# Sixteen early expert products in whole fp32, some of them issued between the groups of the gates

## The chip, the cores and the metric

The kernel runs on one core of a Trainium2 chip. The metric is the device time of one execution in microseconds; smaller is better. The program is one launch with about 49,000 instructions.

## The reference

The reference is a stack of two blocks, each applied with two layers, on 256 tokens of width 1024. Only the second half of a layer of the first block matters here, the product-key expert network (PEER). `h` are the normed tokens:

```python
q = (ht @ w_q).reshape(n_tok, PEER_HEADS, PEER_QDIM)      # 8 heads, 256 wide
s1 = einsum('thd,kd->thk', q[..., :half], sub_keys[0])    # 128 keys each
s2 = einsum('thd,kd->thk', q[..., half:], sub_keys[1])
# best 16 of each, best 16 of their 256 sums: 128 experts (key1*128+key2) for a token
gate = softmax(top)
act = gelu(einsum('td,thkd->thk', hc, expert_u[ec]))
y = einsum('thk,thkd->td', gate * act, expert_v[ec])
```

There are 128 x 128 experts. Each has a row of 1024 in `expert_u` and one in `expert_v`.

## The kernel before

The kernel gathers nothing. It computes a dense matrix of gates, `G` (expert by token, zero where an expert wasn't chosen), and then goes through all 128 blocks of 128 experts in each of the two layers. For a block `i` it computes the activations of all 256 tokens on TensorE (PE), applies gelu on ScalarE (ACT), multiplies with `G` on VectorE (DVE), and adds the product with the block of `expert_v` to `y_ps` in PSUM, where it stays over all blocks.

In the block loop every fp32 operand is split into a high part (fp32r) and a low part (the rest), and a product is three passes, high by high, high by low and low by high. So a block has these steps:

- `u_high` (ACT, line 1950) and `u_low` (DVE, line 2686) split the block of u, into one of two places of `utr`.
- `activations` (PE, line 1318): 8 parts of the width by 3 passes, 24 matmuls of 256 columns into one of two banks `prob_ps`.
- `gelu` (ACT, line 1967) and `weighted` (DVE, lines 2700 to 2704): gate, and the split into `wtr`.
- `v_high` (ACT, line 1977) and `v_low` (DVE, line 2711) split the block of v into `vr`.
- `combine` (PE, line 1330): 12 matmuls of 512 columns.

On PE the order is written out: activations of block i+1 stand ahead of combine of block i. The raw blocks are loaded by SyncE (SP), 512 KB each, into two places for u (`expert_u`) and two for v (`expert_v`), all four in the first half of the tile `slab`. SP waits for the low part of the last user of a place (`next_u`, `next_v`, `next_pair`).

Ahead of that loop come, in this order, the queries and scores of the heads, the search for the best keys on DVE, and the gates. The gates are made in 32 groups of 8 tokens: DVE writes the 8 gated one-hot rows and 1 plain one, POOL 4 plain ones and ACT 3 (`one_hot`, lines 1929 and 1931), PE multiplies them (line 1303, 8 fp32 matmuls of 128 columns, each seen as 2 records), and ACT copies the result to `G` (`gates_out`, line 1939). The rows and the result have two buffers. What DVE, POOL and ACT write for group n+2 waits until group n is full.

`EARLY = (0, 12)`: in layer 1 the activations of the first 12 blocks are made in another way. They are whole fp32 products, 8 matmuls of 256 columns each (line 1290, 16 records), without a split of u and h. Eleven of them stand on PE while DVE is still searching for the best keys, the twelfth stands behind the turning of the pairs (`turn_pairs`) and ahead of the gates. Gelu (line 1900) writes them to small tiles in `slab`, and behind the gates only the combines of these blocks are left, eleven of them in a row. v of blocks 1 and 3 have places of their own (`first_v`), the others share the two places. Layer 0 makes no product early; it starts its loop behind the gates.

In layer 0 PE computes the last two pieces of the modulation (line 1268) ahead of `turn_pairs`.

Of the kernel before, what the change touches and what calls it, by code (L numbers as in the profile page):

```python
# [1 line left out]

# [13 lines left out]
P = 128  # L16
D = 1024
S = 256
# [40 lines left out]
EARLY = (0, 12)  # L59

# [171 lines left out]
def two_blocks(nc, io, out):  # L232
    ctx = ExitStack()
    with ctx:
# [69 lines left out]
        ut_act = Signal(sem("ut_act"), a=NKEYS)  # L304
        ut_dve = Signal(sem("ut_dve"), a=NKEYS)
        am_full = Signal(sem("am_full"), a=NKEYS)
        gelu_done = Signal(sem("gelu_done"), a=NKEYS)
# [3 lines left out]
        v_in = [Signal(sem(f"v_in{q}"), a=NKEYS // PLACES, step=16) for q in range(PLACES)]  # L311
# [4 lines left out]
        early_in = [sem(f"early_in{q}") for q in range(EARLY[1] // 2)]  # L316
        early_full, early_done = sem("early_full"), sem("early_done")
        first_v_in = {i: sem(f"first_v_in{i}") for i in (1, 3)}
# [35 lines left out]
        small = sb("small", [P, 1024])  # L354
# [16 lines left out]
        first_v = {1: hT[:].rearrange("p k s -> p (k s)")[:, D:2 * D], 3: slab[:, 1, D:2 * D]}  # L371

        def early(i):

            at = 3 * D + i * S if i < 4 else (i - 4) * S
            return slab[:, 0, at:at + S]
# [7 lines left out]
        def v_raw(l, i, m):  # L384

            return first_v[i] if isinstance(i, int) and EARLY[l] and i in first_v else expert_v[:, m % 2]

        def v_landed(l, i, m, place):

            if isinstance(i, int) and EARLY[l] and i in first_v:  # L390
                return first_v_in[i], 16
            return v_in[m % 2].at("a", l, place + 1 - (2 if EARLY[l] and m % 2 else 0))
# [30 lines left out]
        assert sr.at <= 1024  # L423
# [50 lines left out]
        early_u = rb.take(EARLY[1] - 4, D)  # L474

        def early_rows(i):

            return early_u[:, i] if i < EARLY[1] - 4 else early_more[:, i - EARLY[1] + 4]
# [188 lines left out]
        def slabs_a(sp, l):  # L667
            if l == 0:
                sp.dma_start(cT, io["c_turned"]).then_inc(c_in, 16)
            for i, name in enumerate(SLABS["a"][l]):  # L670
# [6 lines left out]
                if l == 0:  # L677
# [7 lines left out]
                    if name == "wq3":  # L685
                        sp.wait_ge(t5_out, 16)
                        for h in range(8):
                            for t in range(T):
                                sp.dma_start(skewed[:, h, t, :],
                                             bass.AP(t5_dram.tensor, h * 512 + (P if t == 0 else 0), [[1, P], [1, S]]))\  # L690
                                    .then_inc(t5_skew, 16)
                    for s in {"ada3": (0,), "in1": (1, 2), "in3": (3, 4), "out1": (5, 6, 7), "wq3": (8,)}.get(name, ()):
# [3 lines left out]
            u = io["peer_u"][l]  # L696
            v = io["peer_v"][l].rearrange("(n p) d -> n p d", p=P)
            for q in range(EARLY[l] // 2):
                rows_q = early_u[:, 2 * q:2 * q + 2] if 2 * q < EARLY[l] - 4 else early_more[:, 2 * q - EARLY[l] + 4:][:, 0:2]
                sp.dma_start(rows_q, u[2 * q:2 * q + 2].rearrange("q p d -> p q d")).then_inc(early_in[q], 16)  # L700
            sp.wait_ge(*accs.full_at("a", l, "wq2"))
            sp.sem_inc(passed["sp"], 1)
            for q in range(PLACES):
                if not EARLY[l]:
                    sp.dma_start(expert_u[:, q], u[q]).then_inc(u_in[q].sem, 16)
                if q == 0 or not EARLY[l]:
                    sp.dma_start(expert_v[:, q], v[q]).then_inc(v_in[q].sem, 16)
            if EARLY[l]:
                sp.wait_ge(early_full, EARLY[l])
                sp.sem_inc(passed["sp"], 1)  # L710
                sp.dma_start(first_v[1], v[1]).then_inc(first_v_in[1], 16)
                sp.wait_ge(*gates_full.at("a", l, S // TOKG))
# [2388 lines left out]
```

## Time and profile before

| | |
|---|---|
| three timed runs | 3085.27, 3090.32, 3091.12 us |
| their median | 3090.32 us |
| profiled execution, first to last instruction | 3090.2 us |
| profiled execution, its own time beside the span | not recorded; the span is taken for it |
| PE, DVE, ACT, POOL busy | 96%, 64%, 43%, 9% |
| gates of layer 0 | 281.1 to 364.6 us |
| blocks of layer 0 | 364.7 to 1094.8 us |
| gates of layer 1 | 1344.6 to 1427.2 us |
| blocks of layer 1 | 1429.8 to 2119 us |

How to read it: times in rows are microseconds from the first instruction of the profiled execution. PE is the matmul side of TensorE, PEld its weight loads, which overlap; PEclk is the granted clock as a share of 2.4 GHz. A matmul's record reaches from its start to its modelled end, so that records of matmuls that follow each other overlap; the step from one to the next is the start of the next less its own. The chain follows the last instruction back to what released each, and its pieces abut.

### The profile page before, as it was taken

The numbers are of one execution on the slowest core, as the hardware profiler recorded it, in microseconds if no ns is written. First come the engines' busy times: TensorE is split into PE (matmuls) and PEld (weight loads), VectorE is DVE, ScalarE is ACT, GpSimd is POOL, SyncE is SP. The second block draws the span as 40 slices with busy tenths as digits, with TensorE's granted clock in tenths as the row PEclk, the third lists the DMA queues.
The fourth block names the chain that finished last, engine by engine and source line by source line (L and its number), as shares of the span: only waits on it lengthen the run. The fifth ranks groups of instructions, "written<-read, shape, count | busy, mean of one in ns | idle before, by whom it ended". The sixth has DMA issues, their size and how long they took to land.

```text
span 3090.2 us, 49370 instructions
## 1 busy us (share of the span) xinstructions
PE 2954.5 (96%) x17506; PEld 2574.5 (83%) x17506; DVE 1979.7 (64%) x3642; ACT 1319.7 (43%) x2114; POOL 274.9 (9%) x398
## 2 busy tenths in 40 slices
PE   8897899999999999988999999998999999999999
PEld 4684799999999876877999999998978898988897
DVE  4769866677777634797666666665656655555764
ACT  1245844444444412566444444444443434434433
POOL 0027600000000000473000000000000000000000
PEclk9899999999999998999999999999999999999999
DMA  8532156767666642303555565565334454423454
GB/s 328 199 115 82 54 185 219 234 227 231 225 231 231 211 149 82 144 8 97 190 185 185 196 195 192 189 195 190 108 133 164 162 179 155 176 109 143 160 181 150
DMA packets 130809, 524.33 MB, mean 170 GB/s; under 512 B 17981, under 2 KB 28093, under 8 KB 108025
## 3 DMA queue, kind: packets, MB, share of 16 engines
q1 hardware_dynamic: 120648, 508.13, 47.8%
q10 hardware_dynamic: 10034, 14.52, 1.4%
q8 instruction: 78, 1.28, 0.2%
q14 instruction: 49, 0.40, 0.0%
HBM read 519.44 MB, written 3.16 MB: 169 GB/s over the span
## 4 chain that ended last, share of the span: by engine, by line
PE 81%; DVE 8%; ACT 6%; DMA 1%; issue 1%; DVEq 1%; ACTq 1%; POOL 0%; SPq 0%
PE prob_ps L1318 22%; PE acc L1330 22%; PE acc L966 6%; PE acc L1549 6%; PE acc L1562 6%; PE acc L951 3%; PE acc L925 2%; PE acc L1496 2%; ACT arena L1939 2%; PE turn_ps L1074 2%; PE acc L904 2%; PE acc L1521 1%; ACT arena L1929 1%; PE acc L1048 1%; ACT slab L1931 1%
## 5 line engine op out<-in xcount | busy, mean ns | idle before, releaser
L1318 PEld LDWEIGHTS prob_ps<-hTr,utr 128*128 128x128 f32 x5856 | 734.4, 191 | 26.1 <-issue 8.3
L1318 PE MATMUL prob_ps<-hTr,utr 128*128 128x256 f32 x5856 | 745.5, 284 | 1.7 <-DVE utr L2686 1.2
L1330 PE MATMUL acc<-vr,wtr 128*128 128x512 f32 x2964 | 718.9, 391 | 1.2 <-DVE vr L2711 1.2
L1330 PEld LDWEIGHTS acc<-vr,wtr 128*128 128x128 f32 x2964 | 541.1, 189 | 104.3 <-issue 1.8
L2711 DVE TENSOR_TENSOR vr<-slab,vr 128x1024 fp32r<-128x1024 f32 x246 | 301.4, 1225 | 406.8 <-ACT vr L1977 406.6
L1977 ACT CAST vr<-slab 128x1024 fp32r<-128x1024 f32 x246 | 258.3, 1050 | 578.8 <-PE acc L1330 570.2
L2686 DVE TENSOR_TENSOR utr<-slab,utr 128x1024 fp32r<-128x1024 f32 x244 | 297.3, 1218 | 12.9 <-ACT utr L1950 12.9
L2240 POOL TENSOR_TENSOR small<-small 128x1 f32<-128x1 f32 (+4 forms) x29 | 26.2, 904 | 2666.2 <-DVE small L2303 1459.0
L1950 ACT CAST utr<-slab 128x1024 fp32r<-128x1024 f32 x244 | 255.5, 1047 | 8.2 <-DMA slab<-in_peer_u 3.4
L2961 DVE TENSOR_TENSOR slab_lo<-slab,w_hi 128x2048 fp32r<-128x2048 f32 x64 | 143.8, 2288 | 122.2 <-ACT w_hi L2206 122.2
L2206 ACT CAST w_hi<-slab 128x2048 fp32r<-128x2048 f32 x64 | 119.2, 1908 | 157.9 <-DMA slab<-in_pack_b 149.9
L1967 ACT ACTIVATE arena<-prob_ps 128x256 f32<-128x256 f32 x244 | 93.9, 385 | 209.8 <-PE prob_ps L1318 209.7
L2786 DVE TENSOR_TENSOR slab_r<-slab,arena_r 128x2048 fp32r<-128x2048 f32 (+1 forms) x52 | 115.7, 2258 | 86.7 <-ACT arena_r L2058 86.6
L1303 PE MATMUL acc<-slab 128*128 128x128 f32 x1024 | 130.2, 281 | 37.2 <-ACT slab L1931 29.6
L925 PE MATMUL acc<-hT,slab 128*128 128x256 f32 x704 | 159.5, 383 | 2.7 <-ACT hT L1598 1.4
L1562 PE MATMUL acc<-w_hi,uTr 128*128 128x512 f32 x512 | 157.8, 389 | 2.3 <-issue 2.3
L1303 PEld LDWEIGHTS acc<-slab 128*128 128x128 f32 x1024 | 120.4, 193 | 47.3 <-DVE slab L2679 43.4
L2263 POOL TENSOR_SCALAR slab<-iota,arena 128x128 f32<-128x128 f32 x256 | 152.9, 613 | 45.7 <-ACT arena L1604 32.7
L2675 DVE TENSOR_SCALAR slab<-iota,arena 128x128 f32<-128x128 f32 x512 | 152.9, 368 | 2.2 <-PE acc L1303 2.0
L925 PEld LDWEIGHTS acc<-hT,slab 128*128 128x128 f32 x704 | 132.7, 192 | 21.6 <-issue 3.6
L2350 DVE SCALAR_TENSOR_TENSOR arena<-arena,small 128x512 f32<-128x512 f32 x152 | 113.9, 749 | 16.6 <-DMA arena<-in_pack_a 8.4
L966 PE MATMUL acc<-arena_r,hT_hi 128*128 128x512 f32 (+2 forms) x320 | 122.8, 384 | 0.0
(310 smaller groups left out, 4179.4 us busy)
## 6 DMA issues: line engine op xcount, KB each, us to landing
slab<-in_pack_b SPq DMA_DIRECT2D x132, 1024.0 KB, 4.9
slab<-in_peer_v SPq DMA_DIRECT2D x255, 512.0 KB, 3.5
slab<-in_peer_u SPq DMA_DIRECT2D x244, 512.0 KB, 4.6
arena<-in_pack_a SPq DMA_DIRECT2D x84, 512.0 KB, 4.7
slab<-in_pack_a SPq DMA_DIRECT2D x40, 1024.0 KB, 7.0
arena<-in_peer_u SPq DMA_DIRECT2D x6, 1024.0 KB, 14.6
slab<-in_pack_b SPq DMA_DIRECT2D x4, 832.0 KB, 5.3
arena<-in_pack_a SPq DMA_DIRECT2D x2, 1024.0 KB, 18.3
```

What stands on the lines that cost most here:

```text
L925: ins = pe.matmul(dst, w(k, a, P), lhs[:, k, :], start=(k == 0), stop=(k == KD - 1))
L966: ins = pe.matmul(dst[:, t, 0:n], hT_r[hp][:, 4 * h + k, t * P:t * P + P], proj_operand(u0 + h, wp)[:, k, a:a + n], start=(h == 0 and k == ...
L1303: ins = pe.matmul(gate_ps[:, n % 2, q * P:q * P + P], rows[:, n % 2, 1, q, :], rows[:, n % 2, 0, q, :], start=True, stop=True)
L1318: ins = pe.matmul(prob_ps[:, m % 2, 0:S], utr[:, m % 2, uh, k * P:k * P + P], hTr[:, hh, k, :], start=(k == 0 and n == 0), stop=(k == KD - ...
L1330: ins = pe.matmul(y_ps[:, t, n, :], wtr[:, m % 2, wh, t * P:t * P + P], v[:, vh, n * 512:n * 512 + 512], start=first and k == 0, stop=last ...
L1549: ins = pe.matmul(acc[:, accs.buf("b", use), 2 * h + j, :], mlp_operand(u, wp)[:, k, j * P:j * P + P], hm_r[hp][:, k, :], start=(k == 0 an ...
L1562: ins = pe.matmul(acc_nat(accs.buf("b", f"dn{n}"))[:, t, :], uTr[:, up, 4 * j + k, t * P:t * P + P], mlp_operand(u, wp)[:, k, :], start=(j ...
L1950: act.copy(utr[:, m % 2, 0], expert_u[:, m % 2]).then_inc(ut_act.sem, 1)
L1977: act.copy(v_place(l, i)[:, 0], v_raw(l, i, m)).then_inc(v_hi.sem, 1)
L2263: ins = nc.gpsimd.tensor_scalar(rows[:, n % 2, 1, q, :], iota[:], pairsT[:, 1, tok:tok + 1], None, ALU.is_equal)
L2686: dve.tensor_tensor(utr[:, m % 2, 1], expert_u[:, m % 2], utr[:, m % 2, 0].bitcast(F32), ALU.subtract).then_inc(ut_dve.sem, 1)
L2711: dve.tensor_tensor(v_hl[:, 1], v_raw(l, i, m), v_hl[:, 0].bitcast(F32), ALU.subtract)\
```

## The change

`EARLY` becomes (12, 16): both layers make the activations of their first blocks as whole fp32 products. `AHEAD = (3, 12)` of them stand ahead of the gates. The last one (11 and 15) stands behind the gates. The rest, 8 in layer 0 and 3 in layer 1, are issued matmul by matmul behind the groups of the gates: 64 matmuls over 32 groups, two for each, and 24 over 32 (`gate_steps`). ACT does the gelu of such a block once its last matmul is issued, in the next group.

`LISTED = (0, 12)` blocks of u are loaded ahead in a list, as before; further ones go one by one through the two places of `expert_u`, each when the product two before it is done. The results of gelu have a tile of their own, `early_at`, for which the tile `small` is cut and the scratch for dynamic DMAs made smaller. The high and low parts of v of the early blocks alternate between both places of `utr`, but for the last, which goes to `vr`. For the raw v, the two places of `expert_u` are lent while the early blocks are combined, so that v has four places; only block `EARLY - 2` goes to place i % 2 of `expert_v`. All combines of early blocks stand in a row on PE, and the activations of the next block behind them.

The core of the diff:

```diff
-EARLY = (0, 12)
+EARLY = (12, 16)
+LISTED = (0, 12)
+AHEAD = (3, 12)
+def gate_steps(l, n):
+    total = (EARLY[l] - 1 - AHEAD[l]) * KD
+    return range(n * total // (S // TOKG), (n + 1) * total // (S // TOKG))
...
+        def v_home(l, i):
+            return i % 2 if i == EARLY[l] - 2 else i % 4
...
         def v_place(l, i):
-            if not isinstance(i, int) or i >= EARLY[l] or i % 2 and i != 3:
+            if not isinstance(i, int) or i >= EARLY[l] - 1:
                 return vr[:]
-            return utr[:, 0] if i == 3 else utr[:, 1]
+            return utr[:, 0] if i % 2 else utr[:, 1]
...
SyncE
+            def first_blocks(l):
+                sp.wait_ge(*accs.full_at("a", l, "wq2"))
+                sp.sem_inc(passed["sp"], 1)
+                for q in range(PLACES):
+                    sp.dma_start(expert_u[:, q], u[LISTED[l] + q]).then_inc(u_in[q].sem, 16)
+                for q in range(PLACES):
+                    sp.dma_start(expert_v[:, q], v[q]).then_inc(v_in[q].sem, 16)
...
+            for i in range(LISTED[l] + 2, EARLY[l]):
+                sp.wait_ge(*early_full.at("a", l, i - 1))
+                sp.sem_inc(passed["sp"], 1)
+                sp.dma_start(expert_u[:, i % 2], u[i]).then_inc(u_in[i % 2].sem, 16)
...
+            for i in (2, 3):
+                sp.wait_ge(*early_full.at("a", l, EARLY[l] - 3 + i))
+                sp.sem_inc(passed["sp"], 1)
+                sp.dma_start(expert_u[:, i - 2], v[i]).then_inc(lent_in[i - 2].sem, 16)
+
+            def early_v(i):
+                home = v_home(l, i)
+                sp.wait_ge(*v_lo.at("a", l, i - 3 if i != EARLY[l] - 2 else i - 1))
...
+            def first_u(i, k):
+                sp.wait_ge(*v_lo.at("a", l, k))
...
+            for i in range(4, EARLY[l] - 2):
+                early_v(i)
+            first_u(EARLY[l], EARLY[l] - 5)
+            early_v(EARLY[l] - 1)
+            early_v(EARLY[l] - 2)
+            next_v(EARLY[l], 0)
+            first_u(EARLY[l] + 1, EARLY[l])
...
TensorE
+                for i in range(AHEAD[l]):
+                    if i == AHEAD[l] - 1:
                         turn_pairs()
...
+                    early_products(i)
...
                     ins.then_inc(gates_full.sem, 1)
+                    for i, steps in groupby(gate_steps(l, n), lambda step: AHEAD[l] + step // KD):
+                        early_products(i, [step % KD for step in steps])
+                early_products(EARLY[l] - 1)
...
+                for i in range(EARLY[l]):
+                    combine(i, i, first=i == 0)
+                activations(EARLY[l], EARLY[l])
+                for i in range(EARLY[l], EARLY[l] + 2):
+                    activations(i + 1, i + 1)
+                    combine(i, i)
...
ScalarE
                 one_hot(0)
                 for n in range(S // TOKG):
                     if n + 1 < S // TOKG:
                         one_hot(n + 1)
+                    if n == 0:
+                        early_gelu(AHEAD[l] - 1)
+                    else:
+                        ended(n - 1)
                     gates_out(n)
+                ended(S // TOKG - 1)
...
+                for i in range(EARLY[l]):
+                    v_high(i, i, i // 2)
+                    if i == 1:
+                        early_gelu(EARLY[l] - 1)
+                u_high(EARLY[l], EARLY[l], EARLY[l] // 2)
...
VectorE
+                for i in range(EARLY[l]):
+                    weighted(i, i)
+                    v_low(i, i)
+                u_low(EARLY[l], EARLY[l])
```

In layer 0 SP issues `first_blocks` ahead of the last pieces of the modulation, in layer 1 behind the list of early u. The numbers of repeats of the block loops follow from `EARLY`.

## Rows read from the trace of the kernel before

**Rows 1.** The page: busy time of each engine and share of the span.
```profile
PE 2954.5 (96%) x17506; PEld 2574.5 (83%) x17506; DVE 1979.7 (64%) x3642; ACT 1319.7 (43%) x2114; POOL 274.9 (9%) x398
```
**Rows 2.** The page: the chain that ended last, shares by line.
```profile
PE prob_ps L1318 22%; PE acc L1330 22%; PE acc L966 6%; PE acc L1549 6%; PE acc L1562 6%; PE acc L951 3%; PE acc L925 2%; PE acc L1496 2%; ACT arena L1939 2%; PE turn_ps L1074 2%; PE acc L904 2%; PE acc L1521 1%; ACT arena L1929 1%; PE acc L1048 1%; ACT slab L1931 1%
```
**Rows 3.** The chain in time, block loop of layer 0: start, us, what.
```profile
401.88 2.87 PE prob_ps L1318 x24
404.75 2.75 PE acc L1330 x12
```
**Rows 4.** The chain in time, gates of layer 0 and the start of its blocks.
```profile
281.10 3.38 PE acc L1303 x16
...
307.55 1.01 ACT arena L1939
...
310.11 1.01 ACT arena L1939
...
364.67 3.13 PE prob_ps L1318 x24
...
373.78 2.87 PE prob_ps L1318 x24
```
**Rows 5.** Windows: busy time of each engine in the gates of layer 0.
```profile
285.00:361.00 76.00, 59.91 (x476) 55.04 (x474) 76.00 (x269) 71.75 (x150) 71.31 (x120) 1.00 0.01 1
```
**Rows 6.** Timeline of PE, a gate group; in brackets the idle time before it.
```profile
310.29 2.02 PE L1303 MATMUL acc<-slab 128*128 128x128 f32 x16 [0.54 <-ACT slab L1931]
```
**Rows 7.** Timeline of PE ahead of the gates, layer 0 and layer 1.
```profile
262.32 7.13 PE L1268 MATMUL prob_ps<-arena 128*128 128x512 f32 x16
275.84 1.84 PE L979 MATMUL turn_ps<-ident,arena 128*128 128x128 f32 x6 [6.38 <-DVE arena L1635]
281.10 5.15 PE L1303 MATMUL acc<-slab 128*128 128x128 f32 x32 [3.42 <-DVE slab L2679]
...
1297.52 38.42 PE L1290 MATMUL prob_ps<-hT,arena 128*128 128x256 f32 x176
...
1344.55 3.73 PE L1303 MATMUL acc<-slab 128*128 128x128 f32 x32
```
**Rows 8.** Timeline behind the gates of layer 1, all engines.
```profile
1426.15 1.01 ACT L1939 COPY arena<-acc 128x1024 f32<-128x1024 f32 x1 [1.23 <-PE acc L1303]
...
1427.20 0.42 DVE L2697 TENSOR_TENSOR arena<-slab,arena 128x256 f32<-128x256 f32 x1 [3.80 <-ACT arena L1939]
...
1428.41 1.22 DVE L2711 TENSOR_TENSOR utr<-slab,utr 128x1024 fp32r<-128x1024 f32 x1
...
1429.77 4.56 PE L1330 MATMUL acc<-utr,wtr 128*128 128x512 f32 x12 [3.65 <-DVE utr L2711]
...
1434.13 2.96 PE L1330 MATMUL acc<-vr,wtr 128*128 128x512 f32 x12
```
**Rows 9.** The chain in time behind the gates of layer 1.
```profile
1439.74 3.42 DMA slab<-in_peer_v
...
1443.17 1.06 ACT vr L1977
...
1451.43 4.78 DMA slab<-in_peer_v
...
1464.38 2.87 PE prob_ps L1318 x24
```
**Rows 10.** Windows where the granted clock (third number from the end) is low.
```profile
270.00:281.00 11.00, 1.81 (x6) 1.01 (x6) 9.09 (x24) 3.32 (x10) 3.11 (x6) 0.67 0.06 25
...
1430.00:1437.00 7.00, 7.00 (x24) 5.31 (x24) 4.13 (x7) 1.05 (x1) 0.00 (x0) 0.76 0.25 75
```
**Rows 11.** Timeline of ACT: a gelu and the instruction after it.
```profile
367.82 0.38 ACT L1967 ACTIVATE arena<-prob_ps 128x256 f32<-128x256 f32 x1 [1.01 <-PE prob_ps L1318]
368.10 1.04 ACT L1977 CAST vr<-slab 128x1024 fp32r<-128x1024 f32 x1
```
**Rows 12.** The page: issues of loads of u, median us from issue to landing.
```profile
slab<-in_peer_u SPq DMA_DIRECT2D x244, 512.0 KB, 4.6
```

More of the change, by code:

```diff
@@ L1 @@
 from contextlib import ExitStack
+from itertools import groupby
 import numpy as np
@@ L370, in two_blocks, with lent, v_raw, v_landed @@
         expert_v = slab[:, 0, 2 * D:4 * D].rearrange("p (q d) -> p q d", q=PLACES)
-        first_v = {1: hT[:].rearrange("p k s -> p (k s)")[:, D:2 * D], 3: slab[:, 1, D:2 * D]}
         def early(i):
-            at = 3 * D + i * S if i < 4 else (i - 4) * S
-            return slab[:, 0, at:at + S]
+            return early_at[:, i]
+        def v_home(l, i):
+            return i % 2 if i == EARLY[l] - 2 else i % 4
+        def lent(l, i, q):
+            return sum(v_home(l, j) == 2 + q for j in range(min(i, EARLY[l])))
+        def v_raw(l, i, m):
+            if isinstance(i, int) and i < EARLY[l] and v_home(l, i) >= 2:
+                return expert_u[:, m % 2]
+            return expert_v[:, m % 2]
+        def v_landed(l, i, m, place):
+            first = i if isinstance(i, int) else EARLY[l]
+            if first < EARLY[l] and v_home(l, i) >= 2:
+                return lent_in[m % 2].at("a", l, lent(l, i + 1, m % 2))
+            return v_in[m % 2].at("a", l, place + 1 - lent(l, first, m % 2))
         def v_place(l, i):
-            if not isinstance(i, int) or i >= EARLY[l] or i % 2 and i != 3:
+            if not isinstance(i, int) or i >= EARLY[l] - 1:
                 return vr[:]
-            return utr[:, 0] if i == 3 else utr[:, 1]
[L384 to L392, printed above, removed]
+            return utr[:, 0] if i % 2 else utr[:, 1]
         last_v = utr[:, 0]
@@ L1364, in _ @@
                 else:
-                    with pe.Fori(0, PLAIN // 4) as it:
-                        four(it * 4 + 3)
+                    with pe.Fori(0, (PLAIN - EARLY[l]) // 4) as it:
+                        four(it * 4 + (EARLY[l] + 3))
                     pe.wait_ge(tiles_clear, 2)
@@ L1942, in u_high, with ended @@
                 def u_high(i, m, place):
-                    act.wait_ge(*u_in[m % 2].at("a", l, place + 1 - EARLY[l] // 2))
+                    act.wait_ge(*u_in[m % 2].at("a", l, place + 1 - LISTED[l] // 2))
                     if not (isinstance(i, int) and i < EARLY[l] + 2):
                         act.wait_ge(*am_full.at("a", l, i - 1 - EARLY[l]))
-                    elif i == EARLY[l] + 1 and EARLY[l]:
-                        act.wait_ge(*v_used.at("a", l, EARLY[l] - 1))
+                    else:
+                        act.wait_ge(*v_used.at("a", l, i - 2))
                     act.copy(utr[:, m % 2, 0], expert_u[:, m % 2]).then_inc(ut_act.sem, 1)
+                def ended(n):
+                    for step in gate_steps(l, n):
+                        if step % KD == KD - 1:
+                            early_gelu(AHEAD[l] + step // KD)
                 one_hot(0)
@@ L2731, in _ @@
                 else:
-                    with dve.Fori(0, PLAIN // 4 - 1) as it:
-                        four(it * 4 + 3)
+                    with dve.Fori(0, (PLAIN - EARLY[l]) // 4 - 1) as it:
+                        four(it * 4 + (EARLY[l] + 3))
                     dve.drain()
```

184 lines of the change are left out of this document (77 added, 107 removed).

## The prediction

> **What bounds the kernel now.** I read the page first. TensorE (PE) is busy 96% of the span [rows 1], and the chain that ended last runs through PE for most of it: lines 1318 and 1330, the activations and the combination of the expert blocks, are 22% each [rows 2]. So anything that takes matmuls out of the block loop pays, if they go where PE waits. The chain of one block in the loop then gives the price: 2.87 us for the 24 matmuls of activations, 2.75 us for the 12 of combine, with nothing between them [rows 3]. A block costs 5.62 us and PE alone sets it.
>
> Next the chain around the gates, since this is where matmuls are moved to. From 281.10 to 364.67 in layer 0 (and in the same way from 1344.55 to 1426.15 in layer 1) the chain is on ACT: it comes back to the same copy every 2.56 us [rows 4]. In a stretch of 76 us of it DVE is busy for all 76, ACT for 71.75, POOL for 71.3 and PE only for 59.9 [rows 5]. A PE group shows 2.02 us and 0.54 us idle; two groups run without a gap take 3.73 us including the tail of the last matmul, so a group really occupies PE for 1.80 us (which is also its piece in the chain) and leaves 0.76 us [rows 6, 7]. DVE, too, has no room: it makes nine of the rows of a group and needs the 2.56 us for them. Last I read the start of the combinations in layer 1, where the early blocks are used up: PE starts at 1429.77, 3.65 us after the last group of gates, the first combine takes 4.36 us to the start of the next where later ones take 2.75, and then the chain three times goes through a load of v: 3.42 us of DMA, 1.06 us of ACT and the 1.22 us of DVE [rows 8, 9]. The granted clock was 0.76 in 1430 to 1437: part of it at 1.2 GHz, after PE had been idle for 3.65 us [rows 8, 10].
>
> **What a product costs.** A whole fp32 product of one block is 8 matmuls, seen as 16 records. Layer 1 already has eleven in a row: 176 records in 38.42 us, less a tail of about 0.2 us, is 3.46 us a block, 0.432 us a matmul [rows 7]. The same product in the loop costs 2.87 us. So a block made early costs PE 0.59 us more, and the change only pays by where it puts it. The Trainium skill, "FP8 and Floating Point Precision", section "TensorE Precision Notes", says that true fp32 takes four passes through the array; this speaks against the change. With the issue gap of "TensorE: Matmul & The Clock Gate" (Back-to-back issue gap; N/2.4 + 2.5 ns) it would be an estimate of 3.49 us against 2.62 us for three passes, and the sum below would come out 4 us less favourable. The trace shows 3.46 and 2.87, and I go by it.
>
> **Layer 0, ahead of the gates.** Three products now stand here. PE ends the matmuls of the modulation at 269.45 and is idle for 6.38 us until DVE delivers the pairs at 275.84 [rows 7]. Products 0 and 1 take 2 x 3.46 = 6.9 us and end at 276.4: the turn of the pairs is 0.55 us late. Their operands, u of blocks 0 and 1, are now loaded before the pieces of the modulation instead of behind them, and should have landed. Product 2 comes behind the turn and takes 3.46 us, where PE was idle for 3.42 us [rows 7]. The first group so starts at about 281.7 instead of 281.10. It no longer starts at a granted clock of 0.67 [rows 10] (it took 3.38 us [rows 4]); that shortens the start but not the loop behind it.
>
> **Layer 0, between the gates.** 8 products, 64 matmuls, 2 behind each of 32 groups: 0.864 us. PE then needs 1.80 + 0.864 = 2.664 us a group against the 2.56 us of ACT and DVE. ACT gets a gelu every fourth group. A gelu shows 0.38 us, but the next instruction starts 0.28 us after it [rows 11], so four groups are 4 x 2.56 + 0.28 = 10.5 us of ACT against 10.66 us of PE. PE becomes the bound by a little. Does the ring of two buffers hold? Rows of group n+2 start when group n is full (2.0 us after its start) and take 2.56 us: 4.6 us, and PE wants them after 5.33 us. ACT's copy and one-hot rows give the same 4.6 us, or 4.9 us with a gelu. There is room. Below, the price of a group can't be under 2.56 (ACT, DVE); above, it is 2.56 + 0.864 = 3.42 if nothing overlaps. I take 2.664, since PE's records abut elsewhere through waits that were met in time. 32 x 2.664 = 85.2 us: 366.9. Loads of u (512 KB, 4.6 us to landing [rows 12]) have four groups for each, and the queues carry nearly nothing in this stage; behind them on SP stand only later expert loads.
>
> **Layer 0, behind the gates.** Product 11 follows at once: 370.4. Meanwhile copy (1.01), weighting and low half (2.6 us from the copy's end to the start of PE, as in layer 1 [rows 8]) are done at about 370, so this product costs PE only some 0.5 us of its own. Without that cover it would cost 3.46. In the kernel before, PE had done two activations and one combine by 373.78 [rows 4]; taken back by 2 x 2.87 + 2.75, this is a start at 365.3. So the block work starts 370.4 - 365.3 = 5.1 us later, with 12 x 2.87 = 34.4 us less in it.
>
> **The twelve combines in a row.** DVE's part of a block, weighting and low half, runs from 1427.20 to 1429.63 [rows 8], so 2.5 us from the end of combine i-2 with the signal; PE gives it 2.75. v now has four places instead of about two. Its load waits for block i-4 and so has about 8 us for 3.42 to 4.78 us [rows 9]. Two loads are late next. Block 10 is diverted to place 0, behind block 8: 3.42 + 1.06 + 1.22 and gaps is 5.9 us against two combines, 5.5 us: 0.4 us of stall. And u of block 13 waits for the low half of v of block 11; up to 4.6 us [rows 12], 1.06 and 1.22 against 2.75 + 2.87 = 5.62 us and a lead of 0.4: some 0.7 us. I take 1.1 us a layer. From below it is 0; from above, with v at the 4.78 us that one load took in this stage [rows 9], 2.5 us. Sum of layer 0: 34.4 - 5.1 - 1.1 = 28.2 us less.
>
> **Layer 1.** Twelve products stand ahead of the gates as before. Three lie between them: 24 matmuls, at most one behind a group, 0.43 us into 0.76 us of room. ACT stays the bound and gets three gelus: +0.84 us. The last product, 15, covers what was idle: last group (to about 1425.9), 0.84, one matmul 0.43, 3.46: PE starts to combine at 1430.6 instead of 1429.77, +0.9 us, and without a gap, thus at the full clock. Four blocks leave the loop: 4 x 2.87 = 11.5 us. From 1429.77 to the first activations at 1464.38 eleven combines took 34.6 us where 11 x 2.75 = 30.25; the 4.4 us over (1.6 of clock in the first one, the rest waits for v) fall away, and 1.1 us of the two late loads come in: 11.5 + 4.4 - 0.9 - 1.1 = 13.9 us less.
>
> **The sum.** 28.2 + 13.9 = 42.1 us off the profiled 3090.2: 3048. That execution's span is within 0.2 us of the median of the runs, 3090.32, so it is not corrected. The blocks that remain, 116 and 112 of them, run the same loops and keep 5.62 us. The moves of tiles, and the smaller scratch, cost nothing on any row.
>
> **Rivals.** (1) The products don't overlap with the gates: each step delays the next group in full. The 0.54 us of PE idle is ended by ACT or DVE [rows 6], and DVE has no slack to catch up after one slip, which speaks for it; that the ring leaves 0.7 us speaks against. Price: 24.3 us in layer 0 (3.42 for 2.664), 9.5 in layer 1: 3082. Half of it gives 3065. (2) The combines in a row starve for v. Before, two blocks took 5.8 us that way and once 7.2 [rows 9]; now 28 blocks stand in a row. At 3.6 us for 2.75 this is 23 us: 3071; at 2.92 it is 5 us: 3053. For it: 512 KB every 2.75 us is asked, with issue and landing on the path; against: four places, and the same rate is carried in the loop. (3) Slower: in layer 0 the ring degenerates into one buffer, so that DVE's 2.56 us, PE's 2.02 us and the 0.86 us of products follow each other: 5.44 us a group, +89 us: about 3137. It decides from 3.97 us a group in layer 0 ((42.1 us / 32) above 2.664). Against it, PE would have to release the rows of n+2 only when it wants n+1. (4) The saving is given back: the loop is then not bound by PE after all, or the two layers' later stages wait for something else that ends when it did: 3090. The loop shows PE without idle; little speaks for it.
>
> **Chances.** Forecast 0.68, with its own range 3040 to 3058: the loop at 2.56 and no stalls takes 6 off, two layers of full stalls (2.8) and 0.1 us more for each of 64 groups (6.4) give 9 to 10. Rival 1: 0.10, rival 2: 0.12, rival 3: 0.06, rival 4: 0.04. The range 3040 to 3066 takes in the forecast, the milder halves of rivals 1 and 2, and leaves out under 2 in 10. What this measurement can tell from no change is 0.2%, 6 us: faster 0.90, same 0.04, slower 0.06.
>
> **What would show it.** In the profile after: the gates of layer 0 with 2.66 us from group to group, chain on PE; those of layer 1 still 2.56 to 2.6 on ACT; PE without the 6.4, 3.4 and 3.65 us gaps and with a granted clock of 1.00 there; twelve and sixteen combines at 2.75 us, with one gap of half a microsecond near the last but one and another before the second activations; 5.62 us in the loops; and 228 x 24 matmuls of activations for 244 x 24. Wrong would be: groups of 3 us and more, DMA in the chain at each combine, or a loop with gaps.

## The result, and the profile after

| | before | changed |
|---|---|---|
| first comparison, median (runs) | 3089.72 us (4) | 3041.57 us, 3039.56 to 3045.64 (4) |
| ratio | | 0.9839, 95% interval 0.9825 to 0.9852 |
| second comparison, median (runs) | 3091.63 us (9) | 3045.22 us, 3041.36 to 3048.02 (4) |
| ratio | | 0.9853, 95% interval 0.9838 to 0.9868 |
| first profiled execution, span | 3090.2 us | 3043.9 us |
| its own time | not recorded | 3045.64 us |

The change makes the kernel faster by 48 us in the one comparison and 46 us in the other, 1.5 to 1.6%; 42 us were forecast. The first profile, page of the changed kernel, busy time and chain by line, beside [rows 1, 2]:

```profile
PE 2950.1 (97%) x17378; PEld 2563.1 (84%) x17378; DVE 1965.7 (65%) x3626; ACT 1302.8 (43%) x2098; POOL 274.5 (9%) x398
...
PE acc L1385 23%; PE prob_ps L1373 22%; PE acc L1009 7%; PE acc L1597 6%; PE acc L1610 6%; PE acc L994 3%; PE acc L968 2%; PE acc L1355 2%; PE acc L1544 2%; PE turn_ps L1117 2%; PE prob_ps L1336 2%; PE acc L1569 1%; PE acc L947 1%; PE acc L1091 1%; PE acc L1248 1%
```

The lines have moved: combine is line 1385, activations 1373, the early products 1336, the gates 1355. PE has as much work as before (2950 us for 2954), in a shorter span: 2 points of line 1355 and 2 of 1336 stand in the chain where ACT's gates stood. The work was not reduced. It was moved to where PE waited.

The chain in time, gates of layer 0 and what follows, beside [rows 4]:

```profile
270.85 7.14 PE prob_ps L1336 x32
278.00 0.66 PE turn_ps L1022 x6
278.65 3.46 PE prob_ps L1336 x16
...
282.17 2.02 PE acc L1355 x16
284.19 0.87 PE prob_ps L1336 x4
285.06 1.78 PE acc L1355 x16
286.84 0.87 PE prob_ps L1336 x4
287.71 1.78 PE acc L1355 x16
...
366.34 4.32 PE prob_ps L1336 x20
370.66 31.25 PE acc L1385 x132
...
401.98 3.01 PE acc L1385 x12
404.99 2.87 PE prob_ps L1373 x24
...
407.90 3.11 PE prob_ps L1373 x24
```

From 270.85 to 407.90 this chain holds PE and nothing else but 0.2 us of gaps. A group and its two matmuls take 1.78 + 0.87 = 2.65 us (285.06 to 287.71), the last product is in the 4.32 us at 366.34, and 132 records at 370.66 are eleven combines in a row. The windows say the same of the engines and of the clock, beside [rows 5, 10]: PE, which was busy for 59.91 of 76 us, is now busy for all 76.00, and the granted clock is 1.00 where it was 0.67 and 0.76.

```profile
269.00:282.00 13.00, 12.59 (x58) 10.01 (x56) 10.69 (x26) 5.78 (x13) 2.63 (x5) 1.00 0.27 81
285.00:361.00 76.00, 76.00 (x578) 73.12 (x577) 75.35 (x259) 71.14 (x152) 68.44 (x116) 1.00 0.16 50
...
1402.00:1448.00 46.00, 45.92 (x196) 35.57 (x195) 35.84 (x62) 16.17 (x17) 0.00 (x0) 1.00 0.58 186
```

In layer 1 the gates stay with ACT, and the chain goes over to PE only at their end, beside [rows 8, 9]:

```profile
1386.46 1.01 ACT arena L1986
1387.47 0.30 ACTq L1977
1387.77 0.58 ACT arena L1976 x2
1388.42 0.52 ACT slab L1978
...
1389.02 1.01 ACT arena L1986
...
1396.88 2.02 PE acc L1355 x16
1398.90 3.89 PE prob_ps L1336 x18
1402.79 39.65 PE acc L1385 x168
...
1442.51 5.69 PE acc L1385 x24
1448.19 2.87 PE prob_ps L1373 x24
```

The copy of ACT comes back after 2.56 us (1386.46 to 1389.02). No load of v stands between 1402.79 and 1448.19, and the first combine starts without a gap of PE ahead of it.

Each kernel was profiled three times in all. The second profile of the changed kernel belongs to the second comparison, for which it was expected that the second block takes 962 to 971 us if only the granted clock of an execution sets its length (theory A), or again 966 us or less if the change shortens what follows as well (theory B). It took 962.6 us, which both allow. From the records of the matmuls, us:

| stretch | before | changed | difference of the means |
|---|---|---|---|
| start to the first gates of layer 0 | 281.1, 281.5, 282.8 | 282.2, 283.2, 283.0 | +1.0 |
| first gates to last combine, layer 0 | 815.0, 815.7, 815.1 | 786.9, 786.6, 787.6 | -28.3 |
| between the two, code unchanged | 248.4, 247.4, 252.1 | 248.2, 246.6, 249.3 | -1.3 |
| first gates to first combine, layer 1 | 85.2, 85.2, 85.2 | 85.3, 85.2, 85.3 | 0.0 |
| first to last combine, layer 1 | 689.4, 689.6, 689.4 | 675.5, 675.5, 675.7 | -14.0 |
| second block, code unchanged | 971.1, 968.8, 969.0 | 965.8, 962.6, 969.0 | -3.8 |

The stretches that the change touches give 1.0 - 28.3 - 14.0 = -41.3 us. From the gates on they repeat within 1 us, the start within 1.7 us. The other 5 us of the three profiles lie where the source is the same, and there one and the same kernel differs by up to 6 us between its executions.

### The profile page after: what moved, and what is told of

It reads as the page before. It is cut to its first block, busy times and chain, and to the rows that moved or that the text cites. A ratio compares the mean times of both kernels' runs of the same rounds, so it can differ in the third digit from the quotient of the medians.

```text
span 3043.9 us, 49161 instructions
## 1 busy us (share of the span) xinstructions
PE 2950.1 (97%) x17378; PEld 2563.1 (84%) x17378; DVE 1965.7 (65%) x3626; ACT 1302.8 (43%) x2098; POOL 274.5 (9%) x398
## 4 chain that ended last, share of the span: by engine, by line
PE 86%; DVE 6%; ACT 4%; issue 1%; DMA 1%; DVEq 1%; ACTq 0%; POOL 0%; SPq 0%
PE acc L1385 23%; PE prob_ps L1373 22%; PE acc L1009 7%; PE acc L1597 6%; PE acc L1610 6%; PE acc L994 3%; PE acc L968 2%; PE acc L1355 2%; PE acc L1544 2%; PE turn_ps L1117 2%; PE prob_ps L1336 2%; PE acc L1569 1%; PE acc L947 1%; PE acc L1091 1%; PE acc L1248 1%
## 5 line engine op out<-in xcount | busy, mean ns | idle before, releaser
L1373 PEld LDWEIGHTS prob_ps<-hTr,utr 128*128 128x128 f32 x5472 | 686.3, 191 | 24.5 <-issue 7.9
L1373 PE MATMUL prob_ps<-hTr,utr 128*128 128x256 f32 x5472 | 697.1, 284 | 1.4 <-issue 1.3
L1385 PE MATMUL acc<-vr,wtr 128*128 128x512 f32 x2736 | 663.7, 391 | 0.1
L1385 PEld LDWEIGHTS acc<-vr,wtr 128*128 128x128 f32 x2736 | 499.3, 188 | 94.9 <-issue 0.5
L2767 DVE TENSOR_TENSOR vr<-slab,vr 128x1024 fp32r<-128x1024 f32 x228 | 279.5, 1226 | 367.5 <-ACT vr L2030 367.5
L2030 ACT CAST vr<-slab 128x1024 fp32r<-128x1024 f32 x228 | 239.4, 1050 | 524.2 <-PE acc L1385 524.2
L2742 DVE TENSOR_TENSOR utr<-slab,utr 128x1024 fp32r<-128x1024 f32 x228 | 277.9, 1219 | 13.2 <-ACT utr L1997 13.2
L1997 ACT CAST utr<-slab 128x1024 fp32r<-128x1024 f32 x228 | 238.8, 1047 | 16.4 <-DMA slab<-in_peer_u 10.5
L2021 ACT ACTIVATE arena<-prob_ps 128x256 f32<-128x256 f32 x228 | 87.7, 384 | 205.8 <-PE prob_ps L1373 205.8
```

The source lines that it names most:

```text
L1373: ins = pe.matmul(prob_ps[:, m % 2, 0:S], utr[:, m % 2, uh, k * P:k * P + P], hTr[:, hh, k, :], start=(k == 0 and n == 0), stop=(k == KD - ...
L1385: ins = pe.matmul(y_ps[:, t, n, :], wtr[:, m % 2, wh, t * P:t * P + P], v[:, vh, n * 512:n * 512 + 512], start=first and k == 0, stop=last ...
L1997: act.copy(utr[:, m % 2, 0], expert_u[:, m % 2]).then_inc(ut_act.sem, 1)
L2030: act.copy(v_place(l, i)[:, 0], v_raw(l, i, m)).then_inc(v_hi.sem, 1)
L2742: dve.tensor_tensor(utr[:, m % 2, 1], expert_u[:, m % 2], utr[:, m % 2, 0].bitcast(F32), ALU.subtract).then_inc(ut_dve.sem, 1)
L2767: dve.tensor_tensor(v_hl[:, 1], v_raw(l, i, m), v_hl[:, 0].bitcast(F32), ALU.subtract)\
```

## The experiments

All of them are edits of the changed kernel, unless the text says otherwise. Where two ratios are compared, both come from comparisons with the kernel before on the same chip.

**The kernel before, again.** No edit.

> The kernel before, unchanged, for a second profile of it. The two profiles differ by 41.1 us up to the end of the experts of layer 1 and by another 5.3 us in the second block, whose code is the same: 971.1 us before with 51.8 us of it at half the granted clock, 965.8 us after with 36.0 us. Theory A (the 5.3 us is the granted clock, which falls differently from one execution to the next): the part up to the end of the experts repeats within 1 us (2119), and the second block may come out at another length, between about 960 and 972 us, in step with its time at half clock. Theory B (the change shortens the second block by what it leaves behind): the second block again takes 971 us.

It took 3089.93 us. The end of the experts came at 2119.4 us as expected; the second block took 968.8 us. So the same kernel gave 2.3 of the 5.3 us by itself, which speaks for A but doesn't decide. At half the granted clock it ran for 42.7 us of this block, for 51.8 us in the first profile.

**8 early products in layer 0.**

```diff
-EARLY = (12, 16)
+EARLY = (8, 16)
```

> The changed kernel with 8 early products in layer 0 for 12: 4 between the gates for 8, one matmul behind each group. Theory A (the products between the gates are nearly free until PE is full; a block out of the loop is worth 2.87 us): gates of layer 0 go back to 2.56 us a group plus 4 gelus of 0.28, 83 us for 84.8, and 4 blocks of 2.87 us come back into the loop: 9.7 us more than the changed kernel, about 3051. Rival (the products cost their 3.46 us wherever they stand): 13.8 us of products go, 11.5 come back: 2 us less, about 3039.

Median 3055.74 us, ratio 0.9876 (0.9857 to 0.9894). In the profile the gates up to the first combine take 85.7 us for 88.1, and from the first gates to the last combine of layer 0 795.1 us for the 787.0 of the changed kernel, 8.1 us more, where 9.7 were forecast; the end of layer 1's experts comes 9.6 us later. The chain of this kernel shows what a gelu costs ACT:

```profile
300.45 1.01 ACT arena L1986
...
303.01 1.01 ACT arena L1986
...
305.96 0.90 ACTq L1977
306.86 0.88 ACT arena L1976 x3
308.41 1.01 ACT arena L1986
```

From copy to copy 2.56 us; over the two groups with a gelu between them 308.41 - 303.01 = 5.40 = 2 x 2.56 + 0.28. The chain here is ACT's: with one matmul behind a group PE isn't the bound, as theory A has it. The rival, 2 us less than the changed kernel, is out.

**12 early products in layer 1, none between the gates.** Eleven ahead, one behind.

```diff
-EARLY = (12, 16)
-LISTED = (0, 12)
-AHEAD = (3, 12)
+EARLY = (12, 12)
+LISTED = (0, 10)
+AHEAD = (3, 11)
```

> The changed kernel with layer 1 held at 12 early products as before: 11 ahead of the gates, none between, the twelfth behind them, v with four places as changed. Theory A: 4 x 2.87 = 11.5 us come back, less 0.8 us of gelus and less about 0.4 us that the gates start earlier: 10.3 us more than the changed kernel, about 3052; the first combine stays at the full clock and the 4.4 us of waits and clock at the start of the combines stay away. Rival (what layer 1 gained came from the places of v alone): within 2 us of the changed kernel.

Median 3054.63 us, ratio 0.9874 (0.9858 to 0.9891). First gates to first combine 84.7 us for 85.3, first to last combine 686.8 for 675.5: 11.3 us of the 11.5 came back, and 689.4 - 686.8 = 2.6 us against the kernel before stay, which is what the product behind the gates and the four places of v bring. Both parts are as theory A has them, but the 2.6 are less than the 4.4 - 1.1 of the prediction. The rival, that layer 1 gained by the places of v alone, is out.

**The same products, twice as dense.** 64 matmuls behind the first 16 groups of layer 0.

```diff
-    return range(n * total // (S // TOKG), (n + 1) * total // (S // TOKG))
+    groups = S // TOKG
+    if l == 0:
+        groups //= 2
+    return range(min(n, groups) * total // groups, min(n + 1, groups) * total // groups)
```

> The changed kernel with the same 64 matmuls in layer 0, but four behind each of the first 16 groups of gates and none behind the last 16. Theory A (a group takes the larger of PE's sum and 2.56 us): 16 x (1.78 + 1.73) = 56.2 and 16 x 2.56 = 41.0, 97.1 us for 84.8: 12.3 us more than the changed kernel, about 3054. Rival (the ring of two buffers slips when PE is late, and DVE or ACT don't catch up): the first 16 groups take 4 us and more, 20 us more in all. Second rival (the spread of the products doesn't matter): no difference.

Median 3054.63 us, ratio 0.9881 (0.9862 to 0.9900). From its chain, in the first half:

```profile
302.42 1.78 PE acc L1358 x16
304.21 1.73 PE prob_ps L1339 x8
305.94 1.78 PE acc L1358 x16
```

3.52 us a group, the sum of PE's own parts and no more; in the second half it is ACT's 2.56 again. Without overlap a group of the first half would take 2.56 + 1.73 = 4.29 us. Gates to first combine took 99.98 us for 88.14, 11.8 us more. So the ring does not slip even where PE needs a full microsecond more than the others in every group. Rivals 1 and 3 of the prediction would have shown here first.

**The products of layer 0 ahead of the gates.**

```diff
-AHEAD = (3, 12)
+AHEAD = (11, 12)
```

> The changed kernel with the products of layer 0 that lay between the gates put ahead of them: 11 ahead for 3. Theory A (they are hidden only where PE waits): eight more products stand on the path, each the larger of 3.46 us and half of a load and a product ((4.6 + 0.1 + 3.46) / 2 = 4.1 us, as u goes through two places), 33 us; the gates go back from 2.65 to 2.56 us a group, 3 us less: 30 us more than the changed kernel, about 3071. Rival (where they stand doesn't matter, what counts is that they aren't in the loop): within 3 us of the changed kernel.

Median 3067.72 us, ratio 0.9925 (0.9910 to 0.9940). The timeline of PE:

```profile
278.38 29.16 PE L1336 MATMUL prob_ps<-hT,slab 128*128 128x256 f32 x128 [0.19 <-DMA slab<-in_peer_u]
307.38 0.82 PE L1022 MATMUL turn_ps<-ident,arena 128*128 128x128 f32 x6
308.03 3.62 PE L1336 MATMUL prob_ps<-hT,slab 128*128 128x256 f32 x16
311.72 2.02 PE L1355 MATMUL acc<-slab 128*128 128x128 f32 x16
```

Eight products take 29.0 us, 3.63 each and not the 4.1 estimated from the loads, and the gates start that much later. Against the changed kernel beside it (3045.22 us) the median is 22.5 us longer, where 30 were forecast; by the stretches it is 25. They are back at 84.7 us to the first combine, 3.4 us less. The same eight products cost 3.4 us between the gates and 29 us ahead of them. What they are worth depends on where they stand.

**Another order of the places of v.**

```diff
-            return i % 2 if i == EARLY[l] - 2 else i % 4
+            return (2, 3, 0, 1)[(i - 1) % 4] if i else 0
```

(with the loads and counts that follow from it)

> The changed kernel with another order of the places of v: v of blocks 1 and 2 go to the two lent places, 3 to the first, 4 to the second and so on, so that no load of v waits for the block just before it and u of the block behind the early ones can be loaded three blocks ahead. Theory A (the gaps of the changed kernel behind the early combines are these two late loads): the 1.1 us gap of layer 0 and that of layer 1 ahead of the last early combines, and the 0.2 us ahead of the second activations, go; v of block 2 is late by some 0.4 us instead. From the first combine to the end of the blocks 0.9 us less in each layer, 1.8 in all, about 0.1% on the whole, which the ratio can't tell but the profile can. Rival (the gaps are DVE's, whose part of a block is 2.5 of 2.75 us): they stay.

Median 3048.58 us, ratio 0.9855 (0.9840 to 0.9870), the same as the changed kernel beside it. First to last combine: 699.6 and 676.2 us, for 698.4 and 675.5 in the changed kernel profiled beside it. The edit brought nothing. v of blocks 1 and 2 came late: the first two steps of the row are 1.1 us longer in layer 0 and 0.7 us in layer 1. What the edit removed at the end was less than I had taken it for.

**A third order, without late loads.** The edit is shown against the order before it.

```diff
-            return (2, 3, 0, 1)[(i - 1) % 4] if i else 0
+            return i if i < 4 else (2, 3, 0, 1)[(i - 1) % 4]
```

> The changed kernel (12 and 16 early products) with a third order of the places of v: 0, 1, 2, 3, then 1, 2, 3, 0 in turn, so that v of block 1 is again loaded early (in the order before this one, loads of v of blocks 1 and 2 were on the path: combine 2 stood 1.5 us late), and each place is taken over at least three blocks after its last user. Theory A (a load of v fits in three combines, 8.25 us, and not in two, 5.5 us): twelve and sixteen combines without a gap of over 0.2 us; from the first combine to the end of the blocks 1.3 us less than the changed kernel in each layer: 697.3 us for 698.6 and 674.2 for 675.5. On the whole 0.1%, which the ratio can't tell. Rival: another load, that of u of the second block behind, takes the place of the gap, and the two stretches stay within 0.3 us.

Median 3047.60 us, ratio 0.9859 (0.9838 to 0.9881). First to last combine 698.4 and 675.4 us: still the same, so theory A falls, and the named rival (u of the second block) isn't it either, as PE shows no wait for it. In layer 1 all fifteen steps of the row are now 2.82 to 2.85 us, with no late load among them, and not 2.75. The timeline of the changed kernel in that row of combines shows where the 0.1 us comes from:

```profile
387.39 2.58 PEld L1385 LDWEIGHTS acc<-utr,wtr 128*128 128x128 f32 x12 [0.34 <-issue]
...
390.27 2.61 PEld L1385 LDWEIGHTS acc<-utr,wtr 128*128 128x128 f32 x12 [0.30 <-issue]
390.50 0.43 DVE L2753 TENSOR_TENSOR arena<-early_at,arena 128x256 f32<-128x256 f32 x1 [0.35 <-PE acc L1385]
...
391.71 1.22 DVE L2767 TENSOR_TENSOR utr<-slab,utr 128x1024 fp32r<-128x1024 f32 x1
...
393.05 2.57 PEld L1385 LDWEIGHTS acc<-utr,wtr 128*128 128x128 f32 x12 [0.17 <-issue]
```

A combine begins at 387.39, the next at 390.27, then 393.05. DVE starts the weighting of the block after next at 390.50, 3.1 us after the combine that frees its buffer began; that combine fills 2.75 us of PE, but its records reach to 2.96 us [rows 8], when the last matmul is out. DVE ends the low half at 392.93, and PE starts 0.12 us later (the profile names no releaser for this wait of PE; the same 0.12 us lies ahead of the combines at 387.39 and 390.27). From 387.39 round to 393.05 it is 5.66 us for two blocks, 2.83 a block. Eleven such steps are 31.1 us, and the chain above has 31.3. The gaps are those of the two buffers between PE and DVE, spread over all combines in a row; to the late loads at most 0.3 us a layer are left. This is read from the timeline and from the steps that stay without late loads; no version made DVE's part shorter or gave it a third buffer.

**20 early products in layer 1, first version.** In the first other order.

```diff
-EARLY = (12, 16)
+EARLY = (12, 20)
...
-            return early_at[:, i]
+            if i < OLD_PLACE[l]:
+                return expert_v[:, 1, i * S:i * S + S]
+            return early_at[:, i - OLD_PLACE[l]]
```

> The same order of places, and 20 early products in layer 1 for 16: seven between the gates, 56 matmuls over 32 groups; the first four results of gelu stand in the second place of v, which is then free until the fourth block. Theory A (between the gates of layer 1 PE has 0.76 us a group, of which 1.75 x 0.432 = 0.756 us are now used): gates at 2.56 us a group plus 4 more gelus of 0.28, 1.1 us; four blocks of 2.87 us leave the loop: 10.4 us less than with the order of places alone, 12 us less than the changed kernel, about 3029. Rival (PE and ACT, both full, slip against each other): groups of 2.7 us and more, and half of the gain lost or more.

Median 3038.49 us, ratio 0.9823 (0.9806 to 0.9839), for 0.9855 with 16. The gates run at 2.61 us a group (ACT's own sum with seven gelus is 2.56 + 7 x 0.28 / 32 = 2.62), 87.0 us to the first combine. First to last combine takes 666.9 us, 8.6 less and not 11.5: v of blocks 2 and 4 are late, the chain has two waits for them.

```profile
1405.74 3.61 DMA slab<-in_peer_v
1409.37 1.06 ACT utr L2040
...
1412.97 3.99 DMA slab<-in_peer_v
1416.99 1.06 ACT utr L2040
```

**20 early products in layer 1, second version.** `EARLY` and `OLD_PLACE` as in the first version, in the third order; these lines of it then apply in layer 1.

```diff
+            if OLD_PLACE[l]:
+                return (0, 2, 3, 0, 2, 1)[i] if i < 6 else (2, 3, 0, 1)[(i - 1) % 4]
             return i if i < 4 else (2, 3, 0, 1)[(i - 1) % 4]
```

> That order, with 20 early products in layer 1; the order of places there is 0, 2, 3, 0, 2, 1, 3, 0, 1 and so on, as the second place of v holds four results of gelu until the fourth is weighted, and v of blocks 2 and 4 were late before (combine waited 3 us in all). Theory A: in layer 1 from the first gates to the first combine 87 us as in the run with 20 before this one, for 85.2; from there to the end 675.5 - 11.5 - 1.3 + 0.5 (v of block 2 is still late by half a microsecond) = 663.2 us. With 1.3 us in layer 0, 12 us less than the changed kernel up to the end of the experts; ratio to before 0.981. Rival (PE full between the gates of layer 1 gives back what the blocks bring): 5 us or less.

Median 3041.57 us, ratio 0.9841 (0.9822 to 0.9861), for 3047.60 us and 0.9859 with 16 beside it. In the profile 86.7 us and 664.9 us (87 and 663.2 forecast), one wait for v is left. Over the experts of both layers with their gates it takes 1538.2 us, the changed kernel 1547.2, 1547.6 and 1548.5 in its three profiles: 9.6 us less, where 12 were forecast. The ratios alone, whose intervals overlap, would not show it; the stretches do. It is the fastest version of the study by them, though the first version has the lower ratio.

**Two more profiles.** The kernel before and the changed one, no edit.

> The kernel before a third time, for its profile. Theory A (the second block's length is set by how much of it runs at the half granted clock, which differs between executions): its second block lies on one line with the others (956.3 us + 0.26 us for each us at half clock, fitted to six profiles), anywhere between 962 and 971 us. Theory B (the second block is shorter in the changed kernel as such): again 969 to 971 us.

> The changed kernel a third time, for its profile. Theory A: second block on the same line, between 962 and 971 us. Theory B: 962 to 966 us, as in its two profiles so far. Both: 2077 to 2079 us up to the end of the experts.

3095.42 and 3051.55 us. The second block took 969.0 us in both. The windows of the second block, first of before (first profile), then of changed, changed again and changed a third time:

```profile
2119.16:3090.20 971.04, 925.87 (x5484) 817.94 (x5484) 556.50 (x569) 402.12 (x473) 15.11 (x20) 0.97 0.43 154
```
```profile
2078.02:3043.86 965.84, 920.57 (x5484) 813.18 (x5484) 555.97 (x569) 401.92 (x473) 15.06 (x20) 0.98 0.43 155
```
```profile
2077.01:3039.60 962.59, 915.89 (x5484) 808.34 (x5484) 555.68 (x569) 401.44 (x473) 15.06 (x20) 0.99 0.43 155
```
```profile
2080.76:3049.70 968.94, 926.12 (x5485) 818.92 (x5484) 556.39 (x569) 401.97 (x473) 15.10 (x20) 0.97 0.43 154
```

The same 5484 matmuls, at a mean granted clock of 0.97, 0.98, 0.99 and 0.97. The changed kernel alone covers 962.6 to 969 us, so theory B as it was put, 966 us or less each time, is out. But something of it holds. The chains at the start of the second block, of before (its first profile):

```profile
2121.87 0.41 issue
...
2156.56 1.89 issue
```

and of the changed kernel (its first profile):

```profile
2080.73 0.05 issue
...
2114.03 1.15 issue
```

The same instructions stand on both sides of these gaps, in which the engine waits for nothing that the profile shows. In all three profiles of before the first matmul of the second block comes 0.34 us later after the experts, and the second gap takes 1.80 to 1.89 us; in the three of the changed kernel it is 1.15. So about 1 us of the difference in the second block is there in every one of these profiles, without an edit of its source. Why the gaps differ isn't shown. The same kind of gap stands in layer 1: twice in its gates the kernel before takes 2.84 us for a group in place of 2.56, where no gelu lies; the first of them has a gap of 0.34 us on ACT for 0.07 in the other groups.

**The moment at which the second block begins.** Kernels before and changed with extra matmuls ahead of the activations of the last block, overwritten by them.

```diff
+                    if l == DEPTH - 1 and isinstance(i, int) and i == NKEYS - 1:
+                        for k in range(24):
+                            pe.matmul(prob_ps[:, m % 2, 0:S], utr[:, m % 2, 0, k % KD * P:k % KD * P + P], hTr[:, 0, k % KD, :],
+                                      start=True, stop=True)
```

(24 and 12 in the kernel before, 4 in the changed one)

> The kernel before with 24 more fp32r matmuls of 256 columns ahead of the activations of the last block of layer 1, whose result is overwritten: pure PE work of 2.87 us, so that everything behind begins 2.9 us later. Theory C (the length of the second block, 962.5 us in one form and 968 to 971 in another, hangs on the moment at which it begins; the changed kernel meets the short form more often because its experts end at other moments): end of the experts at 2122 us, second block in the short form, 962 to 964 us: span 3085 us, 3 to 5 us less than before in spite of the added work, and most of its runs with a mean granted clock above those of before. Theory A (the form differs at random from one execution to the next): 969 us as in the three profiles of before, or either form, ratio 1.001.

> The same with 12 matmuls, 1.44 us. Theory C: the second block begins at a moment that no profile has shown yet; it takes some length that repeats in the runs, most likely still the long form, 968 us. Theory A: either form, ratio 1.0005.

> The changed kernel with 4 such matmuls, 0.48 us. Theory C: the moments of the changed kernel at which the second block was short (two of three profiles, 962.6 and 965.8 us) move to those at which it was long: 967 to 970 us in the profile, span about 3048, ratio 0.9865 or above, with mean granted clocks of 0.98 to 0.982. Theory A: either form, ratio 0.985 as measured for the changed kernel.

Medians 3091.65, 3091.77 and 3046.88 us; ratios 0.9998 (0.9986 to 1.0009), 1.0003 (0.9993 to 1.0014) and 0.9858 (0.9838 to 0.9877); second block 969.7, 970.2 and 965.3 us. Theory C missed both where it was definite: the first stayed long, the last did not become long. Added work of 2.9 us could not be seen in the ratio. The stretch from the first to the last combine of layer 1 does show it: 691.5 and 690.7 us for 689.4 to 689.6. And the gap of 1.89 us above is 1.15 us with 24 extra matmuls and 1.43 us with 12: it changes with the instructions ahead of it.

## Why the prediction was right or wrong

Its mechanism held, and so did the sum of its terms for the stages that it works out; the size of the whole was short, by 6 us in the first comparison and 4 in the second. Two of the terms were off and cancelled each other, which was luck.

- **Products 0 to 2 ahead of the gates:** start of the gates +0.6 us forecast, +1.0 measured. PE starts product 0 at 270.85, where I had 269.45. The last piece of the modulation starts 0.6 us later than before, takes 0.4 us more (a load that lands at 264.98 is in the chain), and a gap of 0.41 us follows.
- **Between the gates of layer 0:** 2.664 us forecast, 2.65 measured, bound by PE. The ring holds with room (the dense version). Rivals 1 and 3 are out.
- **Product 11 behind the gates:** PE at 370.4 forecast, 370.66 measured.
- **Combines in a row:** this term was mis-sized, and its cause was wrong. I had DVE's part at 2.5 us of 2.75 and thus no bound, because I counted from the end of a combine's share of PE and not from the end of its last matmul. The step is 2.83 us, 0.08 us over, in 28 combines. I had put 0.4 and 0.7 us a layer on two late loads instead. The next pieces of the chain put the third activations of the loop at 413.90; from 370.66 that is 43.2 us for 41.5 us of work (13 x 2.75 + 2 x 2.87), 1.7 us of gaps for 1.1 forecast; in layer 1 it is 1.8 us, counted in the same way. Rival 2, starving for v, is out.
- **Layer 0:** 28.2 forecast, with the late start in it; measured 28.3 - 1.0 = 27.3.
- **Layer 1:** gates on ACT at 2.56, first combine without a gap at full clock, as forecast. First gates to first combine +0.9 forecast, 0.0 measured; first to last combine -14.8 forecast, -14.0 measured. 13.9 against 14.0 in all, by luck: the 0.9 that did not come paid for the larger gaps. It did not come because only two of the three gelus lie between the groups (2 x 0.28 us; the third stands behind the last copy, at 1399.85), and the kernel before lost as much there in the two groups of 2.84 us.
- **The loops** keep 5.62 us (2.87 + 2.75), as forecast.
- **The sum:** 42.1 forecast, 41.3 in the stretches that it speaks of.
- **The step that failed** is in the sum: "28.2 + 13.9 = 42.1 us off the profiled 3090.2: 3048". It puts everything outside the two gates and block stages at nothing, and gives no reason but that one span agreed with the median of the runs. Measured, the unchanged stages (between the layers, and the second block) are 1.3 + 3.8 = 5.1 us shorter in the means of three profiles each. About 1 us of it are the gaps at the start of the second block, which stand in every profile. The rest differs from execution to execution: the second block lies between 968.8 and 971.1 us in the kernel before and between 962.6 and 969.0 us in the changed one. It stood at 962.5 to 962.7 us in four of twelve profiles of kernels with the change or a version of it, and in none of five of the kernel before, with or without the extra matmuls.
- **The base** was not the fault. A run's time is 1.7 to 2.0 us over its span (3045.64 and 3043.9), so that the profiled execution of before, 3090.2 us of span, was some 2 us longer than the median of the runs; but 42.1 off that median gives the same 3048.

What stays open is whether the short second block is chance or something the changed kernel meets more often. The interval of the first comparison, 46 to 54 us, leaves out the 41.3; that of the second, 41 to 50 us, just holds it. Nine of the ten kernels with the change or a version of it came out lower in the ratio than their stretches alone say (they share five sets of runs of the kernel before), which speaks against chance, and the experiments on the moment of the start did not find a cause.

## What to carry to other kernels

Matmuls taken out of a loop that PE sets are worth what they cost there, if they can be put behind something else: the same eight products cost 3.4 us interleaved with a stage that ACT and DVE set, and 29 us as a block ahead of it. Fill the idle engine only up to the period of the others: the period is the larger of the sums, as long as the buffers give each side a group's time. Where two engines hand two buffers back and forth, as PE and DVE here, count the round trip from the end of the last instruction that reads a buffer, not from the moment its engine takes the next one. And compare the stretches that a change touches, over more than one profile, before a few microseconds of the total are explained; stages whose source is the same are no exception.

## What was not expected of the hardware

The granted clock is at half in parts of the unchanged second block, where it costs: a straight line through fourteen profiles (all but the three with extra matmuls) gives 957 us and 0.24 us for each microsecond at half the clock, with 962.6 us at 25.6 us of it and 969.0 at 53.2. The three profiles of the kernel before lie 1.7 to 1.9 us above that line, so the clock isn't all of the difference. Which of the spells occur differs between executions of one kernel. The total of the kernel before ranged from 3080.3 to 3098.6 us over 23 runs on one chip, 0.6%.

Such spells also stand ahead of the gates of layer 0. Every profile but one has 20 to 27 us at half the clock between 14 and 180 us; that of the second version with 20 early products has none, and its gates start at 272.4 us instead of 283.1 as in the third order. This stretch of it, then of the third order:

```profile
95.00:175.00 80.00, 69.86 (x352) 47.68 (x349) 49.00 (x110) 25.47 (x69) 1.11 (x2) 1.00 0.47 173
```
```profile
95.00:175.00 80.00, 71.76 (x300) 49.18 (x297) 44.06 (x86) 23.73 (x64) 1.12 (x2) 0.83 0.47 173
```

That one execution took 3029.03 us, where the other four of its kernel took 3039.21 to 3044.11. So the 10 us belong to that execution and not to the edit. A profile of one execution can miss the usual time of its kernel by that much.
